# Late routings at six-slot steps, one-hot lists at four-slot steps, V products from group 92, and halved query products in a gather-fed expert stage

## The chip, the cores and the metric

The kernel runs on one core of a Trainium2 chip. The metric is device time in microseconds (us) of one execution. The kernel before took 946.21 us, the median of three runs (945.91 to 949.0).

## The reference, cut to what matters

One decoder layer on 256 tokens of width 1024 in float32: self attention (dilated and block-sparse branches), cross attention, an expert stage, and a final norm. The change is in the expert stage, which is this (heads 8, keys 128, TOPK 16, expert tables of 16384 rows):

```
q = (hf @ w_q).reshape(T, PEER_HEADS, 2, PEER_KEY_DIM // 2)
sc = einsum('thpc,pkc->thpk', q, sub_keys)
v1, i1 = top_k(sc, 16)                  # per half of the key
cand = v1[:, :, 0, :, None] + v1[:, :, 1, None, :]
cidx = i1[:, :, 0, :, None] * 128 + i1[:, :, 1, None, :]
top, pos = top_k(cand, 16)
experts = take_along_axis(cidx, pos)    # 8 heads x 16 experts for each token
gates = softmax(top)
a = gelu(einsum('cd,ced->ce', xc, u[ec]))
y = einsum('ce,ced->cd', gates * a, v[ec])
```

## The kernel before, in words

The first 300 us or so are the attention stages. Then comes the expert stage, which is cut into units, slots and groups. A unit is one head for one tile of 128 tokens (16 units: units 0 to 7 are tile 0). A unit has 16 slots, one for each chosen expert; slot n takes, for every token of the tile, the token's expert row (u and v side by side, 8 KB for each token, 1 MB for a slot) by one indirect DMA that GpSimd issues (line 2385). There are 256 slots. Two slots are a group (128 groups).

A slot goes through these hands. GpSimd waits until the buffer's last user is done (`slot_free`) and issues the gather. VectorE multiplies the u half with the normalised rows and sums it (line 2177, `dot(n)`). ScalarE takes the gelu of a group's two dots, multiplies by the gates and writes two diagonal matrices (lines 1549, 1555 and 1563, `weigh`). TensorE multiplies the diagonals with the v halves, adding into PSUM (`use_pair`, lines 1178 and 1181, with 64x64 tiles), and signals `slot_free`. For the last unit single-slot products are used (lines 1137 and 1300).

The gathers run through a ring of buffers. `ring_order` says which slot uses which buffer. Up to slot 61 there are up to 15 buffers; from `GIVEN_FROM` (62) five are given back for other data. SyncE waits for the last slot in them (`LAST_GIVEN`, line 756) before it sends the expert tables described next.

Experts of the last 20 blocks (of 128 rows each) are not gathered; an index beyond the bound is skipped by the DMA. They are computed densely instead: 20 table blocks of u are multiplied with all tokens' rows (`up_product`, line 1217, groups 37 to 56), and 20 table blocks of v with gated activations (`weigh_block`, line 1249, `DOWN_BEHIND`). The gates for this come from lists: when all routings of a tile are known, TensorE turns the lists (`turn_lists`, lines 1226 and 1227), VectorE splits them (`take_lists`, line 2206 and on), and then for each of 16 chunks of 16 tokens VectorE writes a one-hot array (`onehot`, line 2231), for every second chunk the listed gates (`listed_gates`, lines 2246 and 2251), TensorE multiplies 48 small matrices (`token_gates`, line 1236), ScalarE takes the result (line 1632), and VectorE multiplies it into the activations (`weigh_acts`, line 2260). `weigh_block(0)` waits until all 16 chunks are through. Each v table block is 512 KB, loaded by SyncE when an earlier block has been used; the first five lie ready.

Routing a unit is 15 small VectorE steps (`route_step_of`, lines 1983 to 2055) that are laid behind dots. Which step is behind which slot is written out: `over_slots` for units 1 to 6, `LATE_ROUTES` (first slot of the unit) and `LATE_STEPS` (offset of each step) for units 7 to 15. In late units ScalarE does steps 5, 11 and 15 behind the groups of `RANKS_BEHIND`, `TOP_BEHIND` and `ROWS_BEHIND`. `GATES_AT` says after which slot the gate weights are made.

The query products of heads 3 to 7 are TensorE products of 32 matmuls (`whole_query`, line 836) behind the groups of `QUERY_BEHIND`; two groups later follows `key_score` (line 1147), whose scores routing of that head needs. The score of head 7 is also what SyncE waits for (line 757) before it sends the first u tables.

Programs of all engines are in the order written; an instruction that waits holds all behind it on its engine.

Of the kernel before, what the change touches and what calls it, by code (L numbers as in the profile page):

```python
# [94 lines left out]


EARLY_ROUTED = 6
LATE_ROUTES = {7: 78, 8: 86, 9: 94, 10: 102, 11: 110, 12: 118, 13: 127, 14: 136, 15: 145}
LATE_STEPS = {1: 0, 2: 1, 3: 2, 4: 3, 6: 6, 7: 7, 8: 7, 9: 8, 10: 8, 12: 11, 13: 12, 14: 13}
ROUTE_AT = {}  # L100
for part_of_route in (over_slots(1, 0, 10), over_slots(2, 11, 21), over_slots(3, 29, 39), over_slots(4, 40, 51),
                      over_slots(5, 52, 65), over_slots(6, 66, 79)):
    ROUTE_AT.update(part_of_route)
GATES_AT = {13: 1, 25: 2, 43: 3, 56: 4, 70: 5, 82: 6}
SOFTMAX_BEHIND = {3: 2, 8: 3, 18: 4, 24: 5, 31: 6, 38: 7}
RANKS_BEHIND, TOP_BEHIND, ROWS_BEHIND = {}, {}, {}
for unit, begun in LATE_ROUTES.items():
    for step, at in LATE_STEPS.items():
        ROUTE_AT.setdefault(begun + at, []).append((unit, step))
    RANKS_BEHIND[(begun + 3) // GROUP] = unit  # L110
    TOP_BEHIND[(begun + 8) // GROUP] = unit
    ROWS_BEHIND[(begun + 13) // GROUP] = unit
    GATES_AT[begun + 14] = unit
LAST_ROWS_AT = LATE_ROUTES[UNITS - 1] + 16


TURN_BEHIND = {7: 0, 9: 1}
# [1 line left out]
UP_FROM = 37  # L119
UP_BEHIND = {UP_FROM + b: b for b in range(BLOCKS)}  # L120
TAKE_UP_BEHIND = {UP_FROM + 2 * j + 2: j for j in range(BLOCKS // 2)}
LISTS_BEHIND = {48: 0, 80: 1}
LISTS_AT = {100: 0, 163: 1}
COUNT_AT = 90
ONEHOT_AT = {}
GATHER_GATES_BEHIND = {}
TAKE_GATES_BEHIND = {}
WEIGHTS_AT = {}
for q in range(TOKEN_CHUNKS):
    begun = 114 + 6 * q if q < TOKEN_CHUNKS // 2 else 165 + 7 * (q - TOKEN_CHUNKS // 2) // 2  # L130
    ONEHOT_AT[begun] = q
    GATHER_GATES_BEHIND[(begun + 2) // GROUP] = q
    TAKE_GATES_BEHIND[(begun + 2) // GROUP + 1] = q
    if q % 2:
        WEIGHTS_AT[begun + 8] = q // 2
DOWN_BEHIND = {}
for b in range(BLOCKS):
    DOWN_BEHIND.setdefault(100 + b * 20 // BLOCKS, []).append(b)
PLAIN_GROUPS = (PEER_HEADS * TOPK // GROUP,)
QUERY_BEHIND = {11: 3, 16: 4, 21: 5, 26: 6, 33: 7}  # L140
LAST_SPLIT = PANELS.index("qpeer2")
OWN_PLACE = SPLIT_RING
QUERY_UNITS = PEER_HEADS - QUERIES_FIRST
# [13 lines left out]
FIRST_BUFFERS = [0, 5, 8, 2, 3, 4, 9, 10, 11, 12]  # L157
PRODUCT_BUFFER = 13
JOINS = {22: 14, 24: 15, 58: 6, 67: 7, 79: 1}
GIVEN_BACK, GIVEN_FROM = (10, 11, 12, 14, 15), 62  # L160


def ring_order():
# [62 lines left out]
def product_order():  # L226
# [4 lines left out]
    def add(name, engine):  # L231
        order.append((name, engine))
# [74 lines left out]
    query(2, 1)  # L307

    for i in range(GROUPS):
        if i in QUERY_BEHIND:  # L310
            add(f"qpeer{QUERY_BEHIND[i]}", "act")
        if i - 2 in QUERY_BEHIND:
            add(f"key_score{QUERY_BEHIND[i - 2]}", "act")
        if i in TURN_BEHIND:
            for half in range(2):
                add(f"row_turn{TURN_BEHIND[i]}_{half}", "act")
        if i in UP_BEHIND and UP_BEHIND[i] % 2:
            add(f"up{UP_BEHIND[i] // 2}", "act")
# [40 lines left out]
def build(nc, x_in, mem_in, rel_bias, panels, keys_in, experts, up_in, gain_cols, gain_rows, ident_in,  # L359
          onehot_in, mask_in, iota_in, count_in, out):  # L360
    with ExitStack() as ctx:
# [344 lines left out]
        def _(sp):  # L706
# [45 lines left out]

            sp.wait_ge(product_ready, PLACE["qpeer4"] + 1)
            sp.dma_start(g_final_row, gain_rows[1:2].to_broadcast([P, D])).then_inc(final_row_in, 16)
            sp.wait_ge(slot_free, LAST_GIVEN + 1)
            sp.wait_ge(ffn_sq_ready, 2 * TILES)
            sp.wait_ge(taken["act"], taken_count(f"key_score{PEER_HEADS - 1}"))
            sp.dma_start(count_row[:], count_in.to_broadcast([P, PEER_KEYS])).then_inc(count_in_place, 16)
            for j in range(2 * BLOCKS):
                i = j % len(tables)  # L760
                before = j - len(tables)
                if 0 <= before < BLOCKS and before % 2:
                    sp.wait_ge(product_ready, PLACE[f"up{before // 2}"] + 1)
# [12 lines left out]
        def _(pe):  # L776
# [42 lines left out]
                                           cut(acts_t, slice(None), k, slice(None)), k == 0, k == CHUNKS - 1)  # L819
                mm.then_inc(product_ready, 1)  # L820

            def whole_query(h):

                name = f"qpeer{h}"
                if name in LOADED_EARLY:
                    pe.wait_ge(early_in[name], 16)
                else:
                    i = RAW_LOADED.index(name)
                    pe.wait_ge(panel_in[i % RAW_RING], 16 * (i // RAW_RING + 1))
                w = raw_panel(PANELS.index(name))  # L830
                b = begin(name)
                all_taken("row_turn1_1")
                for blk in range(2):
                    for k in range(CHUNKS):
                        at = k * S + blk * P
                        mm = pe.matmul(b[:, blk * S:(blk + 1) * S], w[:, at:at + P], rowsT[:, k, :],  # L836
                                       start=(k == 0), stop=(k == CHUNKS - 1))
                mm.then_inc(product_ready, 1)

            def tokens_by_channels(name, acts_t):  # L840

# [413 lines left out]
            for i in range(last_unit):  # L1255
                t = i // (GROUPS // TILES)
                if i == 0:
                    query_product(2, 0)
                    for name in LAST_IN_CROSSED:
                        pe.wait_ge(taken[TAKER[name]], taken_count(name))  # L1260
                if i == 4:
                    query_product(2, 1)
                if i in PLAIN_GROUPS:
                    use_group(t, i)
                    pe.wait_ge(crossed_out, 1)
                    first_of_tile = i + 1
                else:
                    use_pair(t, i, i == first_of_tile)
                if i in (0, 5):
                    query_turn(2, i // 5)  # L1270
                if i in (1, 6):
                    query_scores(2, i // 6)
                if i in QUERY_BEHIND:
                    whole_query(QUERY_BEHIND[i])
                if i - 2 in QUERY_BEHIND:
                    key_score(QUERY_BEHIND[i - 2])
                if i in TURN_BEHIND:
                    row_turn(TURN_BEHIND[i])
# [28 lines left out]
        def _(act):  # L1307
# [350 lines left out]
            for i in range((UNITS - 1) * TOPK // GROUP):  # L1658
# [869 lines left out]
```

## Time and profile before

| | |
|---|---|
| median of 3 runs | 946.21 us |
| profiled execution | 948.55 us, of which the span of instructions is 946.8 us |
| TensorE busy | 852.5 us (90%) |
| VectorE busy | 647.8 us (68%) |
| ScalarE busy | 417.6 us (44%) |
| GpSimd busy | 387.2 us (41%) |
| DMA | 303.20 MB, mean 320 GB/s |
| granted TensorE clock, mean | 0.940 |

The span is what lies between the first and the last instruction; the profiled execution's own time is 1.75 us more. Busy shares are means over stages with different limits, so the stretches of the expert stage have to be read one by one. A granted clock of 1.00 is 2.4 GHz, one of 0.50 is 1.2 GHz; a stretch that shows a value between has had both.

### The profile page before, as it was taken

How to read it: one execution, taken by the hardware profiler on the slowest of the kernel's cores; microseconds unless marked ns; L12 is line 12 of the kernel's file. 1: busy time of each engine (PE TensorE's matmuls, PEld its weight loads, DVE VectorE, ACT ScalarE, POOL GpSimd, SP SyncE). 2: the span in 40 equal slices, each digit the busy share in tenths (PEclk: the TensorE clock that was granted, in tenths of full speed). 3: DMA queues.
4: the chain of work that ended last, by engine and by line, in shares of the span. 5: the costliest groups of instructions: out<-in, count | busy, mean ns of one | idle time of the engine just before them, and what ended most of it. 6: DMA issues, size and time to landing. Idle time of an engine off the chain costs nothing.

```text
span 946.8 us, 15680 instructions
## 1 busy us (share of the span) xinstructions
PE 852.5 (90%) x5808; PEld 549.5 (58%) x5808; DVE 647.8 (68%) x1485; ACT 417.6 (44%) x1049; POOL 387.2 (41%) x307
## 2 busy tenths in 40 slices
PE   9999999999988878888779999677897998999997
PEld 8999998899967424444446556333442553333333
DVE  5434685564577876787855787999979775434465
ACT  5534565544664553454434444444452333222252
POOL 1000085150004466465544334455654566444552
PEclk9999999999999879899979999979877788999999
DMA  8897433266328899999999999999999999999995
GB/s 307 236 222 227 175 100 126 90 247 245 138 106 302 317 397 407 399 400 412 347 399 416 416 406 401 371 373 356 325 379 393 381 374 404 418 417 413 405 366 198
DMA packets 55028, 303.20 MB, mean 320 GB/s; under 512 B 11515, under 2 KB 14959, under 8 KB 21777
## 3 DMA queue, kind: packets, MB, share of 16 engines
q0 software_dynamic: 37152, 225.29, 60.2%
q1 hardware_dynamic: 14968, 74.03, 21.5%
q10 hardware_dynamic: 2832, 2.88, 2.1%
q8 instruction: 46, 0.75, 0.3%
q14 instruction: 30, 0.25, 0.1%
HBM read 343.80 MB, written 1.54 MB: 365 GB/s over the span
## 4 chain that ended last, share of the span: by engine, by line
PE 54%; DMA 18%; DVE 16%; issue 5%; ACT 4%; POOL 1%; another core or an unknown queue 1%; POOLq 0%; SPq 0%; DVEq 0%; ACTq 0%
DMA arena<-in_experts,arena 13%; PE y L1178 12%; DVE late_ring L2177 7%; PE ps L792 7%; PE ps L793 7%; PE ps L794 7%; PE y L1249 4%; PE ps L1236 3%; PE ps L836 2%; DMA late_ring<-in_experts,arena 2%; PE y L1137 1%; PE y L1300 1%; PE ps L1217 1%; ACT diag L1563 1%; DMA x<-in_up 1%
## 5 line engine op out<-in xcount | busy, mean ns | idle before, releaser
L2385 POOL DMA_INDIRECT arena<-in_experts,arena x167 | 219.3, 1313 | 170.5 <-PE ps L1181 124.7
L2177 DVE CUSTOM_DVE_ANT_0 late_ring<-arena 128x1024 f32<-128x1024 f32 x178 | 216.7, 1222 | 102.5 <-DMA arena<-in_experts,arena 95.1
L1181 PE MATMUL ps<-arena,diag 64*64 64x512 f32 x824 | 234.5, 697 | 0.2 <-issue 0.2
L1178 PE MATMUL y<-arena,diag 64*64 64x512 f32 x528 | 147.4, 679 | 31.9 <-ACT diag L1563 31.8
L1178 PE MATMUL y<-late_ring,diag 64*64 64x512 f32 x424 | 122.6, 705 | 40.3 <-ACT diag L1563 39.7
L1549 ACT ACTIVATE acts<-dots 128x2 f32<-128x2 f32 x124 | 25.3, 204 | 268.2 <-DVE dots L2177 268.1
L1746 DVE TENSOR_TENSOR w_lo<-raw,w_hi 128x2048 fp32r<-128x2048 f32 x36 | 84.3, 2344 | 70.2 <-ACT w_hi L1329 70.2
L2177 DVE CUSTOM_DVE_ANT_0 late_ring<-late_ring,arena 128x1024 f32<-128x1024 f32 x73 | 89.2, 1222 | 37.5 <-DMA late_ring<-in_experts,arena 26.9
L2385 POOL DMA_INDIRECT late_ring<-in_experts,arena x55 | 71.1, 1292 | 100.2 <-PE ps L1181 90.4
L1178 PEld LDWEIGHTS y<-arena,diag 64*64 64x64 f32 x528 | 35.0, 145 | 112.2 <-ACT diag L1563 56.2
L1178 PEld LDWEIGHTS y<-late_ring,diag 64*64 64x64 f32 x424 | 29.6, 150 | 110.2 <-ACT diag L1563 61.1
L1329 ACT CAST w_hi<-raw 128x2048 fp32r<-128x2048 f32 x37 | 70.7, 1910 | 50.7 <-DMA raw<-in_panels 37.4
L1563 ACT ACTIVATE diag<-ident,acts 128x128 f32<-128x128 f32 x248 | 86.3, 395 | 4.9 <-PE ps L1181 0.8
L792 PE MATMUL ps<-h_hi,w_hi 128*128 128x256 f32 x304 | 86.9, 286 | 0.0
L793 PE MATMUL ps<-h_lo,w_hi 128*128 128x256 f32 x304 | 86.0, 283 | 0.0
L794 PE MATMUL ps<-h_hi,w_lo 128*128 128x256 f32 x304 | 86.0, 283 | 0.0
L2357 POOL TENSOR_SCALAR arena<-arena,row_inv 128x128 f32<-128x128 f32 (+3 forms) x24 | 29.1, 1229 | 115.1 <-DVE row_inv L1814 114.9
L792 PEld LDWEIGHTS ps<-h_hi,w_hi 128*128 128x128 f32 x304 | 58.3, 192 | 2.3 <-issue 1.7
L793 PEld LDWEIGHTS ps<-h_lo,w_hi 128*128 128x128 f32 x304 | 58.3, 192 | 0.0
L794 PEld LDWEIGHTS ps<-h_hi,w_lo 128*128 128x128 f32 x304 | 58.3, 192 | 0.0
L1181 PEld LDWEIGHTS ps<-arena,diag 64*64 64x64 f32 x824 | 56.4, 149 | 0.7 <-issue 0.6
L1555 ACT ACTIVATE acts<-acts,arena 128x1 f32<-128x1 f32 x216 | 52.0, 288 | 4.3
(345 smaller groups left out, 1727.3 us busy)
## 6 DMA issues: line engine op xcount, KB each, us to landing
raw<-in_panels SPq DMA_DIRECT2D x40, 1024.0 KB, 5.0
arena<-in_panels SPq DMA_DIRECT2D x6, 1024.0 KB, 6.9
late_ring<-in_up SPq DMA_DIRECT2D x12, 512.0 KB, 8.5
late_ring<-in_experts SPq DMA_DIRECT2D x12, 512.0 KB, 8.0
x<-in_up SPq DMA_DIRECT2D x8, 512.0 KB, 9.4
x<-in_experts SPq DMA_DIRECT2D x8, 512.0 KB, 7.9
arena<-in_experts,arena POOLq DMA_INDIRECT x167
arena<-line_scratch ACTq DMA_DIRECT2D x8, 320.0 KB, 8.0
```

Of the source, the lines that this page charges most:

```text
L792: pe.matmul(dst, stationary[0], moving[0], start=first, stop=False)
L793: pe.matmul(dst, stationary[0], moving[1], start=False, stop=False)
L794: return pe.matmul(dst, stationary[1], moving[0], start=False, stop=last)
L1178: straight = pe.matmul(y[rows, t, cols], diag[rows, a % DIAGS, rows], slot(a)[rows, down], start=False, stop=False, skip_group_check=True)
L1181: across = pe.matmul(ps[to, half, :], diag[rows, b % DIAGS, rows], slot(b)[rows, down], start=first, stop=False, skip_group_check=True)
L1249: mm = pe.matmul(y[:, t, cols], in_block_acts[:, block, t * P:(t + 1) * P], down[:, cols], start=False, stop=False, skip_group_check=True)
L1329: nc.scalar.copy(split_parts(n)[0], raw_panel(n)).then_inc(w_hi_ready, 1)
L1555: i = nc.scalar.activation(acts[:, s:s + 1], acts[:, s:s + 1], ACT.Copy, scale=gathered_gates(u)[:, s:s + 1])
L1563: i = nc.scalar.activation(diag[:, s % DIAGS, :], ident[:], ACT.Copy, scale=acts[:, s:s + 1])
L1746: nc.vector.tensor_tensor(low, raw_panel(n), high.bitcast(F32), ALU.subtract).then_inc(w_lo_ready, 1)
L2177: i = nc.vector.tensor_tensor_reduce(row if n < len(FIRST_BUFFERS) else products[s % GROUP], row, h_rows[:, u // PEER_HEADS, :], 1.0, 0.0, ...
L2385: nc.gpsimd.indirect_dma_start(out=slot(n), out_offset=None, in_=experts, in_offset=bass.IndirectOffsetOnAxis(ap=expert_rows(u)[:, s:s + 1 ...
```

## The change

Four schedules are altered; no arithmetic is.

1. Late routings (units 7 to 15) begin at slots 77, 83, 89, ... 125, six slots apart, with shorter offsets (the last step at offset 9, before 13). Before they began at 78, 86, ... 145. The groups behind which ScalarE does its part move with them.
2. The lists: turned behind groups 44 and 68 (before 48 and 80), split at slots 93 and 141 (before 100 and 163); the 16 chunks begin at slots 114, 118, ... 174 (before 114, 120, ... 156 and then 165, 168, 172, ... 189).
3. The 20 v blocks lie behind groups 92 to 117, three in four groups (before one behind each of groups 100 to 119).
4. The query products of heads 3 to 7 are cut in halves of 16 matmuls, the first behind a group one earlier than before, the second behind the old one. The scores stay behind the same groups. The five buffers are given back from slot 70 instead of 62, and SyncE waits for them only ahead of the third u table.

```diff
-LATE_ROUTES = {7: 78, 8: 86, 9: 94, 10: 102, 11: 110, 12: 118, 13: 127, 14: 136, 15: 145}
-LATE_STEPS = {1: 0, 2: 1, 3: 2, 4: 3, 6: 6, 7: 7, 8: 7, 9: 8, 10: 8, 12: 11, 13: 12, 14: 13}
+LATE_ROUTES = {unit: 77 + 6 * (unit - EARLY_ROUTED - 1) for unit in range(EARLY_ROUTED + 1, UNITS)}
+LATE_STEPS = {1: 0, 2: 0, 3: 1, 4: 1, 6: 4, 7: 4, 8: 5, 9: 5, 10: 5, 12: 8, 13: 8, 14: 9}
-GATES_AT = {13: 1, 25: 2, 43: 3, 56: 4, 70: 5, 82: 6}
+GATES_AT = {13: 1, 25: 2, 43: 3, 56: 4, 70: 5, 80: 6}
...
-    RANKS_BEHIND[(begun + 3) // GROUP] = unit
-    TOP_BEHIND[(begun + 8) // GROUP] = unit
-    ROWS_BEHIND[(begun + 13) // GROUP] = unit
-    GATES_AT[begun + 14] = unit
-LAST_ROWS_AT = LATE_ROUTES[UNITS - 1] + 16
+    RANKS_BEHIND[(begun + 1) // GROUP] = unit
+    TOP_BEHIND[(begun + 5) // GROUP] = unit
+    ROWS_BEHIND[(begun + 9) // GROUP] = unit
+    GATES_AT[begun + 10] = unit
+LAST_ROWS_AT = LATE_ROUTES[UNITS - 1] + 12
...
-LISTS_BEHIND = {48: 0, 80: 1}
-LISTS_AT = {100: 0, 163: 1}
+LISTS_BEHIND = {44: 0, 68: 1}
+LISTS_AT = {93: 0, 141: 1}
...
-    begun = 114 + 6 * q if q < TOKEN_CHUNKS // 2 else 165 + 7 * (q - TOKEN_CHUNKS // 2) // 2
+    begun = 114 + 4 * q
...
-    DOWN_BEHIND.setdefault(100 + b * 20 // BLOCKS, []).append(b)
+    DOWN_BEHIND.setdefault(92 + b * 27 // BLOCKS, []).append(b)
-QUERY_BEHIND = {11: 3, 16: 4, 21: 5, 26: 6, 33: 7}
+QUERY_BEHIND = {10: 3, 15: 4, 20: 5, 25: 6, 32: 7}
-GIVEN_BACK, GIVEN_FROM = (10, 11, 12, 14, 15), 62
+GIVEN_BACK, GIVEN_FROM = (10, 11, 12, 14, 15), 70
...
-            sp.wait_ge(slot_free, LAST_GIVEN + 1)
...
             for j in range(2 * BLOCKS):
                 i = j % len(tables)
+                if j == TILES:
+                    sp.wait_ge(slot_free, LAST_GIVEN + 1)
...
-            def whole_query(h):
+            def half_query(h, blk):
...
-                b = begin(name)
+                b = bank(name) if blk else begin(name)
                 all_taken("row_turn1_1")
-                for blk in range(2):
-                    for k in range(CHUNKS):
+                for k in range(CHUNKS):
...
-                mm.then_inc(product_ready, 1)
+                if blk:
+                    mm.then_inc(product_ready, 1)
...
                 if i in QUERY_BEHIND:
-                    whole_query(QUERY_BEHIND[i])
-                if i - 2 in QUERY_BEHIND:
-                    key_score(QUERY_BEHIND[i - 2])
+                    half_query(QUERY_BEHIND[i], 0)
+                if i - 1 in QUERY_BEHIND:
+                    half_query(QUERY_BEHIND[i - 1], 1)
+                if i - 3 in QUERY_BEHIND:
+                    key_score(QUERY_BEHIND[i - 3])
```

ScalarE's `take_query` and `take_scores` move by one index as well, so that they stay behind the same groups.

## Rows read from the trace of the kernel before

**Rows 1.** The page, part 2: 40 slices of 23.67 us.
```profile
PEclk9999999999999879899979999979877788999999
GB/s 307 236 222 227 175 100 126 90 247 245 138 106 302 317 397 407 399 400 412 347 399 416 416 406 401 371 373 356 325 379 393 381 374 404 418 417 413 405 366 198
```
**Rows 2.** Busy time by stretch: from:to, length, PE PEld DVE ACT POOL, PEclk, DMA share, GB/s.
```profile
440.00:480.00 40.00, 27.00 (x180) 11.55 (x172) 30.39 (x83) 18.52 (x55) 24.37 (x17) 0.89 0.94 362
480.00:590.00 110.00, 105.25 (x598) 66.88 (x602) 76.94 (x246) 44.98 (x135) 43.45 (x38) 0.98 1.02 412
590.00:646.00 56.00, 43.25 (x344) 21.17 (x344) 55.08 (x158) 25.95 (x84) 27.04 (x21) 0.88 0.96 361
646.00:694.00 48.00, 35.70 (x311) 16.44 (x304) 47.65 (x127) 23.77 (x74) 27.77 (x21) 0.82 0.95 360
694.00:757.00 63.00, 55.14 (x494) 27.97 (x497) 52.60 (x93) 21.77 (x79) 33.60 (x26) 0.76 0.98 380
757.00:801.00 44.00, 39.16 (x368) 19.72 (x360) 30.52 (x48) 14.02 (x50) 28.78 (x21) 0.85 0.97 386
801.00:903.00 102.00, 100.12 (x437) 35.51 (x434) 44.57 (x74) 25.45 (x93) 48.32 (x37) 0.99 1.01 412
```
**Rows 3.** The dots alone (line 2177) by stretch, two instructions for each slot.
```profile
589.90:645.70 55.80, 28.15 (x46) 0.88 0.96 362
645.70:694.40 48.70, 24.31 (x40) 0.82 0.95 359
694.40:756.90 62.50, 32.25 (x54) 0.76 0.98 381
```
**Rows 4.** VectorE's groups of instructions by shape, 589.9 to 684.2 us.
```profile
L2231 DVE TENSOR_TENSOR late_ring<-counts,column_of 128x2048 bf16<-128x2048 bf16 x7 | 8.5, 1216 | 0.0
L2047 DVE TENSOR_TENSOR work<-work,pairs 128x800 f32<-128x800 f32 x5 | 4.9, 989 | 0.0
...
L2260 DVE TENSOR_TENSOR late_ring<-late_ring,gate_sums 128x640 f32<-128x640 f32 x2 | 3.0, 1480 | 0.0
L2251 DVE TENSOR_TENSOR gates_even<-raw,gate_piece 128x640 bf16<-128x640 bf16 x6 | 2.6, 487 | 0.1
...
L2246 DVE TENSOR_TENSOR raw<-raw,row_of 128x640 bf16<-128x640 bf16 x4 | 2.0, 491 | 0.0
```
**Rows 5.** VectorE's waits, 690 to 800 us: in total, times, longest.
```profile
DVE late_ring L2231 <- remote: 4.6, 1, 4.6
DVE late_ring L2231 <- PE ps L1236: 4.5, 1, 4.5
DVE gate_rest L2206 <- PE ps L1227: 3.9, 1, 3.9
```
**Rows 6.** Timeline of TensorE: start, us, line, [idle before <-releaser].
```profile
457.82 7.17 PE L836 MATMUL ps<-rowsT,arena 128*128 128x256 f32 x32
...
481.94 5.07 PE L1217 MATMUL ps<-rowsT,x 128*128 128x256 f32 x16 [5.25 <-DMA x<-in_up]
...
598.76 0.60 PE L1178 MATMUL y<-late_ring,diag 64*64 64x512 f32 x2
...
719.81 1.06 PE L1178 MATMUL y<-late_ring,diag 64*64 64x512 f32 x2
...
726.83 3.19 PE L1236 MATMUL ps<-gates_even,late_ring 128*128 128x20 bf16 x48
```
**Rows 7.** Timeline of GpSimd, behind the query product of head 7.
```profile
467.70 1.05 POOL L2385 DMA_INDIRECT arena<-in_experts,arena  x1 [5.79 <-PE ps L1181]
```
**Rows 8.** The chain that ended last, in order of time, its end.
```profile
902.93 3.63 PE y L1249 x8
906.56 0.58 PE y L1178 x2
908.44 3.63 PE y L1249 x8
912.07 6.87 PE y L1137 x16
```
**Rows 9.** The page, part 3: GpSimd's DMA queue.
```profile
q0 software_dynamic: 37152, 225.29, 60.2%
```
**Rows 10.** Two stretches of 20 us, columns as in rows 2.
```profile
580.00:600.00 20.00, 17.15 (x104) 10.41 (x96) 16.91 (x51) 8.81 (x26) 7.81 (x6) 1.00 1.01 405
...
820.00:840.00 20.00, 20.00 (x93) 6.90 (x91) 7.89 (x15) 4.15 (x15) 9.28 (x8) 1.00 1.02 417
```

More of the change, by code:

```diff
@@ L309, in product_order @@
     for i in range(GROUPS):
-        if i in QUERY_BEHIND:
-            add(f"qpeer{QUERY_BEHIND[i]}", "act")
-        if i - 2 in QUERY_BEHIND:
-            add(f"key_score{QUERY_BEHIND[i - 2]}", "act")
+        if i - 1 in QUERY_BEHIND:
+            add(f"qpeer{QUERY_BEHIND[i - 1]}", "act")
+        if i - 3 in QUERY_BEHIND:
+            add(f"key_score{QUERY_BEHIND[i - 3]}", "act")
         if i in TURN_BEHIND:
@@ L830, in whole_query @@
                 w = raw_panel(PANELS.index(name))
-                b = begin(name)
+                b = bank(name) if blk else begin(name)
                 all_taken("row_turn1_1")
-                for blk in range(2):
-                    for k in range(CHUNKS):
-                        at = k * S + blk * P
-                        mm = pe.matmul(b[:, blk * S:(blk + 1) * S], w[:, at:at + P], rowsT[:, k, :],
-                                       start=(k == 0), stop=(k == CHUNKS - 1))
-                mm.then_inc(product_ready, 1)
+                for k in range(CHUNKS):
+                    at = k * S + blk * P
+                    mm = pe.matmul(b[:, blk * S:(blk + 1) * S], w[:, at:at + P], rowsT[:, k, :],
+                                   start=(k == 0), stop=(k == CHUNKS - 1))
+                if blk:
+                    mm.then_inc(product_ready, 1)
             def tokens_by_channels(name, acts_t):
@@ L1273, in _ @@
                 if i in QUERY_BEHIND:
-                    whole_query(QUERY_BEHIND[i])
-                if i - 2 in QUERY_BEHIND:
-                    key_score(QUERY_BEHIND[i - 2])
+                    half_query(QUERY_BEHIND[i], 0)
+                if i - 1 in QUERY_BEHIND:
+                    half_query(QUERY_BEHIND[i - 1], 1)
+                if i - 3 in QUERY_BEHIND:
+                    key_score(QUERY_BEHIND[i - 3])
                 if i in TURN_BEHIND:
@@ L1680, in _ @@
                     take_scores_tile(2, 1)
-                if i - 2 in QUERY_BEHIND:
-                    take_query(QUERY_BEHIND[i - 2])
                 if i - 3 in QUERY_BEHIND:
-                    take_scores(QUERY_BEHIND[i - 3])
+                    take_query(QUERY_BEHIND[i - 3])
+                if i - 4 in QUERY_BEHIND:
+                    take_scores(QUERY_BEHIND[i - 4])
                 if i in TAKE_TURN_BEHIND:
```

## The prediction

> **What bounds the kernel now.** I read the page's slices first, then busy time by stretch, then the dots alone, then the waits and timelines of the places that stood out. In the slices [rows 1] the gathers run near 400 to 418 GB/s from slice 15 on, with three dents: slice 19 (347), slices 26 to 29 (371, 373, 356, 325), and a long shallow one up to slice 34. The best 20 us show 417 GB/s [rows 10], and I take that as what the transfers can do. The stretches [rows 2] say what stands behind each dent.
> - 440 to 480: 362 GB/s. No engine is full. TensorE is busy 27 of 40 us, the ring is short, and GpSimd waits 5.79 us for buffers behind the query product of head 7 [rows 7], which holds TensorE for 7.17 us [rows 6].
> - 480 to 590: 412 GB/s, TensorE 105 of 110 us. Transfers and TensorE both bind, VectorE does not (77 of 110).
> - 590 to 694: 360 GB/s, and VectorE busy 102.7 of 104 us. VectorE alone binds: dots, routings and lists lie on one another. The gathers lose (1 - 360/417) x 104 = 14 us here.
> - 694 to 757: 380 GB/s, TensorE 55 of 63 us at a granted clock of 0.76, VectorE 52.6. Here VectorE waits 3.9 us for the turned lists and 4.5 us for a one-hot's buffer; another 4.6 us follow [rows 5].
> - 757 to 801: 386 GB/s. 801 to 903: 412 GB/s and TensorE 100 of 102 us. Both bind again. The chain's end is TensorE without a gap: v blocks of 3.63 us and pairs, then the last unit [rows 8].
>
> So time is what the gathers need plus what they lose. One slot is 225.29 MB / 256 = 0.880 MB [rows 9], or 2.14 us at 412 GB/s. A slot can't be faster than this except out of what is already landed.
>
> **Unit prices.** Between 589.9 and 645.7 us there are 46 dot instructions, so slots 114 to 136 (23 slots) took 55.8 us; the next 20 took 48.7 and the next 27 took 62.5 [rows 3]. A dot costs 28.15/23 = 1.22 us, and about 1.135 from start to start, as its neighbours overlap it by 0.08 to 0.09. By the same overlap a one-hot is 1.13 us, listed gates (one product and three, 0.49 each) 1.7, a weighing 1.40 [rows 4]. A chunk of a list is 1.13 + 1.7/2 + 1.40/2 = 2.68 us. In the VectorE-bound part a slot costs (55.8 + 48.7)/43 = 2.43 us. With a chunk each six slots (0.45) and a routing each eight to nine, this leaves 0.85 a slot, 7.1 us for one late routing; its three products over 800 elements alone are 2.7 [rows 4].
>
> **The change part by part.**
>
> *Ring and halved queries (440 to 480).* The halves put 16 matmuls (3.6 us) behind each of two groups instead of 7.17 behind one. With the later give-back, slots 66 to 78 have 11 to 14 slots between reuses of a buffer, before 9 to 11. The most this can return is the whole loss, (1 - 362/417) x 40 = 5.3 us; the least is nothing, as head 7's scores stay behind group 35 and with them the send of the first u table, whose late landing holds TensorE 5.25 us [rows 6]. The SyncE wait that moves behind two tables was over by then anyway. Earlier queries lie where slices show 397 to 412 GB/s [rows 1] and can give little. I take -3, nearer the upper end, because both causes named in the rows are treated.
>
> *More routing between slots 80 and 114.* From slot 114 on there were 5.0 routings left (0.3 of unit 10, 0.7 of unit 11, units 12 to 15). Now 3.3 are left (0.45 of unit 12, 0.87 of 13, units 14 and 15). So 1.7 x 7.1 = 12 us move forward into the stretch where VectorE has 33 us free of 110 [rows 2]: 89 of 110. Costs lie between 0 and 3 us (a pair that gets steps 3, 4, 12 and 13 needs 2.3 + 1.4 + 1.8 = 5.5 us, just the 5.5 of a group there). I take +1, as the gathers are the bound.
>
> *Slots 114 to 136.* Now: 23 dots 26.1, 3.3 routings 23.4, six one-hots 6.8, three listed gates 5.1 and the fixed rows 0.5, two weighings 2.8: 64.7 us. The same count for before is 26.1 + 2.6 x 7.1 + 4.5 + 3.4 + 0.5 + 1.4 = 54.4, against 55.8 measured, so 1.4 go on top: 66. This stretch gets 10 us longer, a VectorE-bound 2.87 us a slot. Bounds: +6 if the gathers' lead at its start hides part, +14 if ScalarE's casts (three places a unit, now two slots from their users instead of three) are late once or more.
>
> *Slots 137 to 183.* Before 48.7 + 62.5 = 111.2 us. No routing is left here. VectorE has 47 dots 53.3, the lists' split 2, ten one-hots 11.3, five listed gates 8.5, six weighings 8.4: 83.5 us, under the gathers' 47 x 2.14 = 100.6. What is late next is the transfer. The waits of 3.9 and 4.5 us go: the lists are turned four to five slots ahead of the split (before two to three), and a one-hot comes five slots behind the group that frees its buffer (the waiting ones had four). Bounds: 111.2 - 97 = -14 with three landed slots used up, and -2.4 if the pace stays at 62.5/27 = 2.31. I take -11, nearer to the transfer's own row. This and the part before make -1.
>
> *v products, slots 184 to 239.* In 757 to 903 the core moved 44 x 386 + 102 x 412 = 59.0 MB [rows 2]. The same at 412 throughout is 143 us against 146, at 417 it is 141.5. TensorE needs 28 pairs x 1.75 (four starts 0.43 apart, [rows 8]) plus 20 x 3.63 = 122 us, and has gaps again. The 4.6 us wait [rows 5] is in this stretch and goes as well. Bounds 0 and -8 (57.1 MB of 56 slots and 15 tables alone are 138.7 us). I take -4.
>
> *The end.* The last unit's products no longer stand behind a 3.63 us block [rows 8]. The last gathers wait on them: 0 to -3.6, I take -1, since the last dots wait for rows.
>
> Sum: -3 + 1 + 10 - 11 - 4 - 1 = -8 us. The profiled execution (span 946.8, its own time 948.55) would become 938.8 and 940.5. The profiled one is 2.3 us above the median of the runs, so the median goes from 946.2 to **938 us**.
>
> **Two rules of the Trainium skill.** GpSimd issued 21 gathers in 27.04 us in the VectorE-bound 590 to 646 and 37 in 48.32 in the calm 801 to 903: 1.29 and 1.31 us each [rows 2]. The Trainium skill, "SBUF — State Buffer" (Door 3 and the warning on SWDGE under it), says that GpSimd can't write DMA descriptors while VectorE runs a two-port operation. By that rule, packing one-hots and routings closer would slow the gathers' issue; these rows show no longer issue where VectorE is full. I give it nothing.
>
> **The rivals.**
> 1. *Slower: the clock falls in the v stretch.* v blocks now leave every fourth group bare, and TensorE waits for rows there. Where TensorE was busy 39 of 44 us the clock was 0.85, and 0.76 in the stretch before it [rows 2]; pairs then take 1.06 instead of 0.60 us each [rows 6]. TensorE's work for groups 92 to 117 is 26 x 1.75 + 20 x 3.63 = 118 us at full clock, the gathers' 52 x 2.14 + 19 = 130. It decides from a mean clock of 118/130 = 0.91 downward. At 0.80, the mean of the two rows, it is 148 us, 18 more than forecast: 956. Against it: with u blocks between pairs and TensorE busy only 17.15 of 20 us the clock was 1.00 [rows 10], and here it would be about 0.9 busy. Chance 0.12. The Trainium skill, "TensorE: Matmul & The Clock Gate" (HAM oscillation), has this mechanism: idle gaps put the array back to half rate. By that rule the time would come out near rival 1's; the rows of 580 to 600 speak against gaps that long.
> 2. *Same: the middle gives back what the end wins.* Landed rows don't help, one-hots still wait for TensorE at five slots (at clock 0.76 two pairs and 48 small matmuls are 2 x 3.5 + 3.2 = 10.2 us of the 10.7 that five slots last), and slots 137 to 183 run at 2.31. Then -2.4 instead of -11, with the rest at -3: about 945. For it: all three waits of [rows 5] are of that kind. Chance 0.16.
> 3. *Much faster.* Every upper bound but one: -5 + 0 + 7 - 12 - 6 - 2 = -18, 928 us. For it: 14 us lost in 590 to 694 alone. Against: the dense stretch makes a loss of its own. Chance 0.18.
>
> That the schedule isn't kept (a routing or list late, so that a later unit's gathers wait) would be seen as GpSimd waiting for expert rows. The last routing ends near slot 135 and is used from slot 240; nothing there is tight.
>
> **How the numbers follow.** The forecast has 0.54, with a range of its own from 930 to 946. With the rivals, 926 to 949 leaves out under 0.2: the clock case above (0.12) and a third of rival 3 below (0.06). What a measurement can tell is 0.3%, 2.8 us. Faster than 943.4: 0.54 x 0.88 + 0.18 + a little of rival 2 = 0.67. Within: 0.18. Slower than 949: 0.15.
>
> **What would show it.** Right, step by step: no wait over 3 us for the query of head 7 and over 400 GB/s in 440 to 470; VectorE near full over slots 114 to 136 only, about 66 us long; slots 137 to 183 in about 100 us with VectorE under 90% and no wait over 3 us for lines 2206 and 2231; slots 184 to 239 at 410 GB/s with a clock of 0.95 or more. Wrong: a clock of 0.8 behind group 92; one-hots waiting over 4 us in several places; or a longer dense stretch, with casts on ScalarE as the releaser.

## The result: 0.4% slower, outside the forecast

The changed kernel takes 951.27 us (median of 16 runs, 948.15 to 956.1), the kernel before 948.0 us on the same chips (16 runs, 943.9 to 952.51). The ratio is 1.0041, 95% interval 1.0025 to 1.0058. The forecast was 938 us, 8 faster. The profiled execution took 950.01 us, its span 948.2.

The page's slices of the changed kernel (23.7 us each), beside [rows 1]:

```profile
PEclk9999999999999999999989999777879799999999
...
GB/s 306 235 203 228 189 98 133 90 229 260 137 109 295 343 421 416 395 417 418 363 409 407 412 410 390 332 297 268 365 410 409 409 407 417 416 412 372 403 375 186
```

Counted from 0, the dent at slice 19 is shallower (363, before 347). The dent of the middle (slices 25 to 28; the prediction's "26 to 29" are the same four) has become much deeper: 332, 297, 268, 365 where there were 371, 373, 356, 325. Behind it all is at 407 to 417 up to slice 35.

To compare two schedules I cut both traces at the same dots, not at the same times: at the starts of the 115th, 138th, 153rd, 185th and 241st dot (slots 114, 137, 152, 184, 240). Busy time by these stretches, first the kernel before, then the changed one (from:to, length, PE PEld DVE ACT POOL, PEclk, DMA share, GB/s):

```profile
590.00:645.70 55.70, 42.95 (x342) 20.92 (x342) 54.78 (x157) 25.65 (x84) 26.74 (x21) 0.88 0.96 362
645.70:684.20 38.50, 29.14 (x272) 14.59 (x264) 38.22 (x107) 17.81 (x57) 23.20 (x18) 0.87 0.93 344
684.20:757.00 72.80, 62.01 (x534) 30.07 (x538) 62.33 (x115) 28.04 (x97) 38.46 (x30) 0.75 0.99 385
757.00:903.30 146.30, 139.58 (x801) 55.39 (x794) 75.09 (x121) 39.73 (x144) 77.10 (x58) 0.95 1.00 404
```

```profile
585.80:653.10 67.30, 53.28 (x421) 27.19 (x420) 66.27 (x180) 32.05 (x97) 31.91 (x23) 0.77 0.88 322
653.10:686.30 33.20, 33.20 (x306) 17.45 (x305) 30.49 (x58) 11.06 (x39) 19.84 (x14) 0.80 0.86 319
686.30:760.10 73.80, 64.47 (x631) 34.39 (x629) 55.77 (x88) 25.55 (x91) 51.22 (x35) 0.84 1.01 408
760.10:905.60 145.50, 131.02 (x607) 44.69 (x608) 69.12 (x112) 38.87 (x142) 71.40 (x56) 0.95 1.00 404
```

The first dot is at 304.7 and 305.6 us, so the two run alike up to there. Then, by slots:

| slots | before | changed | difference | forecast |
|---|---|---|---|---|
| 0 to 113 | 285.3 | 280.2 | -5.1 | -2 |
| 114 to 136 | 55.7 | 67.3 | +11.6 | +10 |
| 137 to 151 | 38.5 | 33.2 | -5.3 | |
| 152 to 183 | 72.8 | 73.8 | +1.0 | |
| (137 to 183) | 111.3 | 107.0 | -4.3 | -11 |
| 184 to 239 | 146.3 | 145.5 | -0.8 | -4 |
| 240 to 254 | 33.4 | 33.5 | +0.1 | -1 |

The fuller stretch came as forecast; what was to pay for it did not. All three waits of [rows 5] are gone. What VectorE still waits for in 690 to 800 us is rows that the gathers have not yet landed, and it waits for them longer: 37.0 us in all. In the kernel before it was 10.4 us.

```profile
DVE late_ring L2177 <- DMA arena<-in_experts,arena: 9.8, 10, 1.2
DVE late_ring L2177 <- DMA late_ring<-in_experts,arena: 0.6, 1, 0.6
```

```profile
DVE late_ring L2180 <- DMA arena<-in_experts,arena: 30.6, 26, 2.0
DVE late_ring L2180 <- DMA late_ring<-in_experts,arena: 6.4, 6, 1.4
```

So 13 us of waits were removed, and waits for rows took their place: slots 152 to 183, which held two of the three, did not get shorter. That is what the experiments are about. Line numbers of the changed kernel are one to three higher (the dot is line 2180).

### The profile page after: what moved, and what is told of

Read it like the earlier page. It is cut to its first block, busy times and chain, and to the rows that moved or that the text cites. A ratio compares the mean times of both kernels' runs of the same rounds, so it can differ in the third digit from the quotient of the medians.

```text
span 948.2 us, 15693 instructions
## 1 busy us (share of the span) xinstructions
PE 853.0 (90%) x5808; PEld 548.6 (58%) x5808; DVE 652.1 (69%) x1485; ACT 415.0 (44%) x1049; POOL 397.2 (42%) x307
## 4 chain that ended last, share of the span: by engine, by line
PE 50%; DMA 24%; DVE 12%; ACT 6%; issue 5%; POOL 3%; POOLq 0%; SPq 0%; DVEq 0%; ACTq 0%
DMA late_ring<-in_experts,arena 11%; PE y L1179 10%; DMA arena<-in_experts,arena 9%; PE ps L793 6%; PE ps L794 6%; PE ps L795 6%; PE ps L1218 6%; DVE late_ring L2180 4%; PE y L1250 3%; DMA late_ring<-in_experts,expert 2%; POOL arena L2388 2%; PE ps L836 2%; DVE w_lo L1749 1%; ACT diag L1566 1%; ACT w_hi L1332 1%
## 5 line engine op out<-in xcount | busy, mean ns | idle before, releaser
L2388 POOL DMA_INDIRECT arena<-in_experts,arena x164 | 226.6, 1382 | 226.6 <-PE ps L1182 181.5
L1179 PE MATMUL y<-arena,diag 64*64 64x512 f32 x784 | 218.5, 685 | 51.1 <-ACT diag L1566 51.0
L1179 PEld LDWEIGHTS y<-arena,diag 64*64 64x64 f32 x784 | 52.0, 147 | 171.5 <-ACT diag L1566 88.1
L1182 PE MATMUL ps<-arena,diag 64*64 64x512 f32 x544 | 145.7, 661 | 0.0
L1749 DVE TENSOR_TENSOR w_lo<-raw,w_hi 128x2048 fp32r<-128x2048 f32 x36 | 84.9, 2360 | 73.7 <-ACT w_hi L1332 73.7
L2180 DVE CUSTOM_DVE_ANT_0 late_ring<-late_ring,arena 128x1024 f32<-128x1024 f32 x75 | 91.8, 1223 | 41.2 <-DMA late_ring<-in_experts,arena 33.7
L1182 PE MATMUL ps<-late_ring,diag 64*64 64x512 f32 x408 | 116.5, 697 | 0.0
L2388 POOL DMA_INDIRECT late_ring<-in_experts,arena x58 | 78.5, 1354 | 34.2 <-PE ps L1182 17.4
L2360 POOL TENSOR_SCALAR arena<-arena,row_inv 128x128 f32<-128x128 f32 (+3 forms) x24 | 25.7, 1084 | 120.2 <-DVE row_inv L1817 119.9
L1179 PE MATMUL y<-late_ring,diag 64*64 64x512 f32 x168 | 44.5, 654 | 18.5 <-ACT diag L1566 18.5
L1250 PE MATMUL y<-late_ring 128*128 128x512 f32 x96 | 45.6, 619 | 0.0
```

The costliest lines, as they stand in the source:

```text
L1179: straight = pe.matmul(y[rows, t, cols], diag[rows, a % DIAGS, rows], slot(a)[rows, down], start=False, stop=False, skip_group_check=True)
L1182: across = pe.matmul(ps[to, half, :], diag[rows, b % DIAGS, rows], slot(b)[rows, down], start=first, stop=False, skip_group_check=True)
L1250: mm = pe.matmul(y[:, t, cols], in_block_acts[:, block, t * P:(t + 1) * P], down[:, cols], start=False, stop=False, skip_group_check=True)
L1749: nc.vector.tensor_tensor(low, raw_panel(n), high.bitcast(F32), ALU.subtract).then_inc(w_lo_ready, 1)
L2180: i = nc.vector.tensor_tensor_reduce(row if n < len(FIRST_BUFFERS) else products[s % GROUP], row, h_rows[:, u // PEER_HEADS, :], 1.0, 0.0, ...
L2388: nc.gpsimd.indirect_dma_start(out=slot(n), out_offset=None, in_=experts, in_offset=bass.IndirectOffsetOnAxis(ap=expert_rows(u)[:, s:s + 1 ...
```

## The experiments

Each ratio is to the kernel before, run on the same chip in the same rounds, with its 95% interval. The changed kernel itself was not run in these rounds, so a comparison with it is one of two ratios, or of stretches. How far two ratios can be trusted is seen from e12 below: its edit brought about none of the waits that it was made for, and it is at 1.0005 where the changed kernel is at 1.0041. Differences of whole times under some 4 us can't be told this way, except between kernels of the same rounds (e7 and e8, e13 and e14). Stretches are from one profiled execution each. Theory D: the density of slots 114 to 136 is the loss. Its rivals are named with each run.

### Front part alone (e1_queries)

The changed kernel with routings, lists and v products as before:

```diff
-LATE_ROUTES = {unit: 77 + 6 * (unit - EARLY_ROUTED - 1) for unit in range(EARLY_ROUTED + 1, UNITS)}
+LATE_ROUTES = {7: 78, 8: 86, 9: 94, 10: 102, 11: 110, 12: 118, 13: 127, 14: 136, 15: 145}
...
-    begun = 114 + 4 * q
+    begun = 114 + 6 * q if q < TOKEN_CHUNKS // 2 else 165 + 7 * (q - TOKEN_CHUNKS // 2) // 2
```

> Theory D (density: the change lost because routings every six slots and list chunks every four lie on one another over slots 114 to 136, and TensorE works off the backlog at a low clock behind it): the halved queries and the later give-back alone are a small gain, 1 to 4 us under the kernel before, as slots up to 114 came 4.2 us earlier in the changed kernel. Theory Q (the front part of the change costs): at or above the kernel before.

946.73 us, ratio 0.9983 (0.9963 to 1.0003). Not clear of no change, but hardly a cost; theory Q is not borne out. Slots 114 to 183 are as before (56.2, 38.6, 72.6 us).

### v products back (e2_v_back)

```diff
-    DOWN_BEHIND.setdefault(92 + b * 27 // BLOCKS, []).append(b)
+    DOWN_BEHIND.setdefault(100 + b * 20 // BLOCKS, []).append(b)
```

> The changed kernel with its v products back behind groups 100 to 119. Theory D: v products from group 92 were no harm, so this is 0 to 4 us slower than the changed kernel, 950 to 955. Theory V (leaving every fourth group bare and starting at 92 is what lost: 4.0 us of transfers are lost over slots 200 to 240 against 1.6 before): 3 us or more faster than the changed kernel, at or under the kernel before.

950.46 us, ratio 1.0023 (1.0000 to 1.0046), which can't be told from the changed kernel's 1.0041. Slots 184 to 239 take 145.5 us, the very number of the changed kernel. Where the v products lie makes neither a gain (my -4) nor a loss (theory V) that can be seen.

### Routings and front part, no lists (e3_routes_queries)

The changed kernel with lists and v products as before.

```diff
-LISTS_AT = {93: 0, 141: 1}
+LISTS_AT = {100: 0, 163: 1}
...
-    begun = 114 + 4 * q
+    begun = 114 + 6 * q if q < TOKEN_CHUNKS // 2 else 165 + 7 * (q - TOKEN_CHUNKS // 2) // 2
```

> The changed kernel with lists and v products as before, so routings every six slots and the queries alone. Theory D: slots 114 to 136 take about 61 us (56 before, 67 changed), slots 137 to 156 are lighter than in both, and the waits of 3.9, 4.5 and 4.6 us stand: 942 to 946. If routings alone are the harm (theory R: ScalarE's casts, VectorE in 80 to 114): at or above the changed kernel.

947.98 us, ratio 0.9990 (0.9967 to 1.0013), 2 us above the expected band. Slots 114 to 136 took 61.8 us (expected 61), 137 to 151 36.6, 152 to 183 72.2. The waits did not stand as expected: in 690 to 805 us VectorE waits once for TensorE, 1.6 us, at line 2234. Theory R, that routings alone are the harm, falls; a gain isn't shown either.

With e1 and e2 this splits the change in two. The routings (e1 to e3) add 5.6 us to slots 114 to 136 and take 2.0 off slots 137 to 151. The lists (e3 to e2) add 5.4 and take 3.0 off. Neither takes anything from slots 152 to 183 (72.6, 72.2, 72.8).

### First chunks sparse (e4_first_sparse)

```diff
-    begun = 114 + 4 * q
+    begun = 114 + 6 * q if q < 4 else 138 + 4 * (q - 4)
...
-    DOWN_BEHIND.setdefault(92 + b * 27 // BLOCKS, []).append(b)
+    DOWN_BEHIND.setdefault(97 + b * 23 // BLOCKS, []).append(b)
```

> The changed kernel with the first four list chunks six slots apart (114 to 132), the others four apart from 138 to 182, v products behind groups 97 to 119. Theory D: slots 114 to 136 take 60 to 62 us and lose 10 us of transfers instead of 15; over all 4 to 7 us faster than the changed kernel, 944 to 947. Theory V or R: no better than the changed kernel by more than 1 us.

944.09 us, ratio 0.9964 (0.9945 to 0.9984). Slots 114 to 136 took 61.8 us instead of 67.3, and what follows is not slower for it: 33.8, 72.8, 145.4. Moving two of six chunks out of the full stretch (the v products moved as well, which e2 shows to be no matter) turns the slower kernel into one faster than before. This is theory D's case, by size too.

### A third of TensorE's list work (e5_one_piece)

```diff
-                    for piece in range(PIECES):
+                    for piece in range(1):
...
```

> The changed kernel, but TensorE multiplies only the first of three gate pieces for the lists (16 small matmuls a chunk, not 48; two thirds of each gate's precision is left out), so a chunk holds TensorE some 1.1 us instead of 3.2. VectorE's work is the same. Theory P (behind slot 137 TensorE's backlog is what delays the buffers): slots 137 to 151 lose 3 us of transfers or less instead of 7.8, slots 114 to 136 stay at 67 us, in all 4 to 7 us faster than the changed kernel. Theory S (only VectorE's excess counts and the ring just refills): slots 137 to 151 still lose 7 us, at most 1 us faster.

947.0 us, ratio 0.9974 (0.9957 to 0.9991), 4 us under the changed kernel by the medians, 6 by the ratios, 3 by the stretches. Slots 114 to 136 are unchanged (67.2), 137 to 151 go from 33.2 to 30.3 us:

```profile
652.40:682.70 30.30, 25.10 (x200) 11.17 (x196) 30.06 (x58) 10.93 (x39) 20.63 (x14) 0.84 0.94 345
```

In the changed kernel TensorE was busy all of these 33.2 us at a clock of 0.80 and VectorE 30.5; now VectorE has 30.06 of 30.3. Theory P is right in kind: behind the full stretch TensorE's backlog matters. But it is 3 us, not 5: of 417 GB/s the stretch still loses 5.2 us of transfers, between theory P's 3 and theory S's 7. Slots 152 to 183 take 73.7 us again, so nothing of TensorE's list work mattered there.

### Less one-hot work on VectorE (e6_no_onehot)

```diff
-                nc.vector.tensor_tensor(onehots[q % 2], counts[:],
+                few = PEER_KEYS if q < 2 else 4
+                nc.vector.tensor_tensor(onehots[q % 2][:, 0:few, :], counts[:, 0:few, :],
```

> The changed kernel, but from the third chunk on VectorE writes only 4 of 128 columns of the one-hot array (the rest of it is left out and stays old), about 1 us less for each of 14 chunks; TensorE's work is the same. Theory P: slots 114 to 136 get 4 us shorter, slots 137 to 151 still lose 6 us or more, as TensorE has the same backlog; about 4 us faster in all. Theory S: both stretches get better, 137 to 151 lose 4 us or less; 7 us faster or more.

947.3 us, ratio 0.9982 (0.9957 to 1.0007). Slots 114 to 136 took 63.1 us, 4.2 less for four one-hots, so each us of VectorE work in this stretch is a us of time. 137 to 151: 31.7. Of the 10 one-hots behind slot 137 the four in this stretch gave 1.5 us, the six in 152 to 183 nothing (74.1). By the stretches it is 5 us faster than the changed kernel, and 137 to 151 still lose 5.8 us of transfers (theory P: about 4, and 6 or more). That is near theory P; the whole time, 6 us faster by the ratios, would not by itself rule out theory S's 7.

### Routings at five slots, two list schedules (e7_routes5_sparse, e8_routes5_dense)

If VectorE's work is dear in slots 114 to 136 and free before, more of the routing belongs before.

```diff
-LATE_ROUTES = {unit: 77 + 6 * (unit - EARLY_ROUTED - 1) for unit in range(EARLY_ROUTED + 1, UNITS)}
-LATE_STEPS = {1: 0, 2: 0, 3: 1, 4: 1, 6: 4, 7: 4, 8: 5, 9: 5, 10: 5, 12: 8, 13: 8, 14: 9}
+LATE_ROUTES = {unit: 77 + 5 * (unit - EARLY_ROUTED - 1) for unit in range(EARLY_ROUTED + 1, UNITS)}
+LATE_STEPS = {1: 0, 2: 0, 3: 1, 4: 1, 6: 4, 7: 4, 8: 5, 9: 5, 10: 5, 12: 8, 13: 8, 14: 8}
...
-    GATES_AT[begun + 10] = unit
+    GATES_AT[begun + 9] = unit
...
-LISTS_BEHIND = {44: 0, 68: 1}
-LISTS_AT = {93: 0, 141: 1}
+LISTS_BEHIND = {44: 0, 64: 1}
+LISTS_AT = {93: 0, 133: 1}
```

e7 has chunks and v products of e4 besides, e8 those of the changed kernel.

> Late routings five slots apart (77 to 117, their last three steps behind one slot), the second list split at slot 133, the first four chunks six slots apart and the others four, v products behind groups 97 to 119. Theory D: VectorE's sum over slots 114 to 136 is 53 us, under before's 54, as the routings move on into slots 80 to 113, which are bound by transfers (lost there: 3 to 5 us). Slots 114 to 136 take 55 us, and the whole is 4 to 7 us faster than with six-slot routings: 938 to 941. Theory R (more routing before 114 costs as much there): 944 or more.

> The changed kernel with late routings five slots apart and the second list split at slot 133; chunks every four slots and v products as in the changed kernel. Theory D: VectorE's sum over slots 114 to 136 is 58 us instead of 65, so it takes 60 us; 5 to 7 us faster than the changed kernel, 944 to 946, and slower than the sparse one of this call by 3 us or more. Theory R: as the changed kernel.

e7: **941.19 us, ratio 0.9903 (0.9879 to 0.9927)**. e8: 945.66 us, ratio 0.9961 (0.9941 to 0.9981). Both came out as theory D expected, e7 0.2 us above its 938 to 941; between the two lie 4.5 us for two chunks. e7 is faster than both kernels. Its four stretches:

```profile
588.60:644.20 55.60, 42.77 (x331) 20.36 (x332) 54.31 (x137) 28.08 (x86) 26.75 (x19) 0.85 0.89 329
644.20:679.60 35.40, 30.89 (x330) 17.05 (x323) 28.68 (x43) 10.61 (x38) 24.38 (x19) 0.95 1.00 409
679.60:751.90 72.30, 65.05 (x629) 34.36 (x628) 59.40 (x93) 24.71 (x88) 45.04 (x32) 0.83 0.98 395
751.90:897.00 145.10, 130.35 (x655) 47.13 (x654) 70.52 (x116) 40.19 (x146) 70.79 (x56) 0.95 1.00 402
```

The first stretch is as short as before, with VectorE at its limit in it alone; the second has the transfers at 409 GB/s. The slots ahead, which got the work, took 282.0 us (280.2 in the changed kernel).

### Three chunks ahead of slot 138 (e11_three_first)

e7 with `begun = 114 + 8 * q if q < 3 else 138 + 4 * (q - 3)` and v products from group 99.

> Routings five slots apart as in the best so far (which has four chunks before slot 138 and is at 0.990 of before), with only three chunks before slot 138 (eight slots apart), thirteen from 138 to 186, v products behind groups 99 to 119. Theory D: VectorE's sum over slots 114 to 136 falls from 53 to 50 us, near the transfers' 49; 1 to 3 us better, 938 to 940. Theory F (what is left there is the ring's own): no better than 941.

941.19 us, ratio 0.9906 (0.9882 to 0.9931): no better than e7. Slots 114 to 136 took 56.1 us with VectorE busy 53.2, only 1.1 less than in e7, where 3 less were expected. The outcome is theory F's (at 53 us of VectorE work the stretch isn't VectorE's any more), but as VectorE's work hardly fell, the run decides little.

### Fewer bytes (e9_half_tables, e10_fewer_rows)

```diff
-                sp.dma_start(tables[i], table).then_inc(table_in[i], 16)
+                cols = slice(0, D if j < BLOCKS else D // 2)
+                sp.dma_start(tables[i][:, cols], table[:, cols]).then_inc(table_in[i], 16)
```

```diff
-                    bounds_check=GATHERED - 1, oob_is_err=False,
+                    bounds_check=GATHERED - 11 * P - 1, oob_is_err=False,
...
```

> The changed kernel, but the 20 v tables are loaded only in their first half of columns (the other half stays as it was and is left out), 3.9 MB less over slots 184 to 239; TensorE multiplies as before. Theory M (transfers set slots 184 to 239, wherever the v products lie): 145.5 us become 136 to 139. Theory E (TensorE or the ring's round trip sets it): 143 or more.

> The changed kernel, but 11 further blocks of experts (10% of the gathered ones) are neither gathered nor weighed (left out), every instruction else the same; a slot moves 0.79 MB, not 0.88. Theory M (slots 152 to 183 and 184 to 239 are bound by transfers): 73.8 becomes 66 to 69 and 145.5 becomes 134 to 138, while slots 114 to 136, bound by VectorE, stay at 67. Theory E: under 2 us less in each.

942.2 us, ratio 0.9900 (0.9862 to 0.9938), and 919.16 us, ratio 0.9671 (0.9641 to 0.9702). Their last stretches, slots 184 to 239 of e9, then slots 114 to 239 of e10:

```profile
762.00:898.30 136.30, 127.36 (x606) 43.97 (x608) 69.11 (x112) 38.95 (x143) 72.59 (x56) 0.97 1.00 399
```

```profile
575.20:642.40 67.20, 57.15 (x440) 29.68 (x439) 66.16 (x180) 33.32 (x101) 33.33 (x24) 0.82 0.87 315
642.40:674.60 32.20, 32.16 (x324) 17.76 (x324) 30.24 (x56) 10.96 (x39) 20.48 (x15) 0.89 0.82 288
674.60:743.00 68.40, 59.94 (x629) 33.63 (x627) 55.55 (x89) 25.33 (x91) 50.88 (x34) 0.90 0.98 383
743.00:877.00 134.00, 124.78 (x590) 43.34 (x591) 68.99 (x112) 38.60 (x141) 73.27 (x56) 0.97 1.00 394
```

Theory M in every number: 136.3 and 134.0 (changed: 145.5), 68.4 (73.8), and 67.2 where VectorE binds (67.3). Slots 152 to 239 follow the bytes. For slots 152 to 183 this rests on e10 alone, and fewer bytes also shorten the way of each single gather; that the transfers' rate is the limit there, and not this way, is argued from a DMA share of 0.98 to 1.01 in most runs.

### Two waits (e12_two_waits)

`begun = 114 + 4 * q - (2 if q in (11, 15) else 0)`: two one-hots nearer to the group that frees their buffer.

> The changed kernel with chunks 11 and 15 two slots early (156 and 172), three slots behind the group that frees their buffer, so that VectorE waits 3 to 5 us for TensorE at each. Theory M: slots 152 to 183 are set by transfers and still take 73 to 74 us, the whole is within 1 us of the changed kernel. Theory W (as I forecast, such waits are lost time): 5 us or more slower there.

950.81 us, ratio 1.0005 (0.9986 to 1.0024), slots 152 to 183 in 72.2 us. Inconclusive: the waits did not arise. In 690 to 800 us VectorE waited for rows (34.4 us) and for nothing of TensorE's. So the waits had to be made certain.

### Certain waits, late and early (e13_waits_late, e14_waits_dense)

e13 waits at gathers 157 and 171, e14 at 119 and 131 instead:

```diff
+                if n in (157, 171):
+                    dve.wait_ge(slot_free, n + 1)
```

> The changed kernel with two added waits of VectorE for TensorE's use of the slot just multiplied, behind slots 157 and 171, each 4 to 6 us long. Theory M (transfers set the pace over slots 152 to 183, a wait of VectorE under the ring's slack is free): slots 152 to 183 take 73 to 76 us, the whole at most 2 us over the changed kernel. Theory W (such waits are lost time, as I forecast): 82 us or more there.

> The changed kernel with the same two waits behind slots 119 and 131, where VectorE binds. Both theories: slots 114 to 136 get 8 to 12 us longer, from 67 to 75 to 79. Theory M: slots 137 to 183 get back at most 3 us of it, so the whole is 6 us or more over the changed kernel.

e13: 952.92 us, ratio 1.0049 (1.0025 to 1.0073), against the changed kernel's 1.0041. e14: 956.24 us, ratio 1.0073 (1.0050 to 1.0096). The waits are there, and larger in e13; first its two, then its slots 152 to 183 (start, us, instruction, [idle before]):

```profile
705.34 1.23 DVE L2180 CUSTOM_DVE_ANT_0 late_ring<-arena 128x1024 f32<-128x1024 f32 x1 [3.70 <-PE ps L1182]
...
740.87 1.23 DVE L2180 CUSTOM_DVE_ANT_0 late_ring<-arena 128x1024 f32<-128x1024 f32 x1 [7.15 <-PE ps L1182]
```

```profile
688.50:762.90 74.40, 64.47 (x598) 34.03 (x601) 55.11 (x89) 24.61 (x88) 44.08 (x31) 0.82 0.95 377
```

10.9 us of waits lengthen this stretch by 0.6 us. They take the place of waits for rows: VectorE waits 5.7 us for rows in this stretch, and 17.3 in the changed kernel. They may not be wholly free: the next 56 slots take 146.6 us (145.5) and slots 240 to 254 35.0 (33.5), 3 us in all in this profile, which is of one of the longer executions (955.46 us); the medians differ by 1.7 us. In e14, 8.9 us of waits (4.46 and 4.39) lengthen slots 114 to 136 by 8.9, from 67.3 to 76.2:

```profile
588.40:664.60 76.20, 56.11 (x438) 28.29 (x440) 66.31 (x180) 32.06 (x98) 31.24 (x23) 0.73 0.80 293
664.60:695.50 30.90, 30.90 (x300) 16.55 (x296) 30.21 (x58) 10.93 (x40) 19.69 (x14) 0.83 0.89 332
```

The stretch behind gives back 2.3 and the next 1.5. That is 3.8 where at most 3 were expected, and the whole is 5 us over the changed kernel by the medians and by the stretches, 3 by the ratios, where 6 or more were expected: a miss in size. The contrast is theory M's all the same: the same kind of wait costs its full length in the one stretch and a twentieth in the other, and e14, with the smaller waits, is 3.3 us slower than e13 in the same rounds.

All stretches by slots, in us, one profiled execution each:

| kernel | 114 to 136 | 137 to 151 | 152 to 183 | 184 to 239 |
|---|---|---|---|---|
| before | 55.7 | 38.5 | 72.8 | 146.3 |
| changed | 67.3 | 33.2 | 73.8 | 145.5 |
| e1, front alone | 56.2 | 38.6 | 72.6 | 144.8 |
| e2, v back | 67.2 | 33.6 | 72.8 | 145.5 |
| e3, routings and front | 61.8 | 36.6 | 72.2 | 145.0 |
| e4, first chunks sparse | 61.8 | 33.8 | 72.8 | 145.4 |
| e5, a third of list work | 67.2 | 30.3 | 73.7 | 145.6 |
| e6, short one-hots | 63.1 | 31.7 | 74.1 | 145.6 |
| e7, five slots, sparse | 55.6 | 35.4 | 72.3 | 145.1 |
| e8, five slots, dense | 61.3 | 34.8 | 72.6 | 146.1 |
| e9, half v tables | 67.2 | 33.5 | 72.9 | 136.3 |
| e10, a tenth fewer rows | 67.2 | 32.2 | 68.4 | 134.0 |
| e11, three first | 56.1 | 34.6 | 73.5 | 144.9 |
| e12, two waits | 67.2 | 34.4 | 72.2 | 145.9 |
| e13, waits late | 67.2 | 34.2 | 74.4 | 146.6 |
| e14, waits dense | 76.2 | 30.9 | 72.3 | 145.5 |

## Why the prediction was wrong

Step by step, as it put them.

**Front, to slot 113 (-3, +1): right in sign, small.** -5.1 in these profiles. GpSimd's wait about head 7's query is 3.42 and 2.55 us in two parts instead of 5.79 [rows 7], and 440 to 480 us is at 386 GB/s (362), not over 400 as foreseen. Ten profiled kernels with these queries and six-slot routings (e10 left aside) take 279.6 to 282.8 us for this part, so one profile is good to some 3 us here, and e1's whole is -1.6 (+-2) us by the ratio. The 12 us of routing moved here cost little if anything: e1, without them, takes 281.5 us, and in the changed kernel 480 to 586 us is at 405 GB/s with VectorE busy 88 of 106 us.

**Slots 114 to 136 (+10): right.** +11.6. The count of VectorE's work made 66 us, 67.3 were measured, and the same recipe gave e3, e4, e8 and e7 within 2 us. For e11 it missed VectorE's busy time by 3. GpSimd took 31.91 us for 23 gathers here, 1.39 each, against 26.74 for 21, 1.27 each, before: the issue did get longer with the closer packing, but GpSimd was busy under half of the stretch, so this set nothing. (Nothing here shows that the one-hots, TENSOR_TENSOR in [rows 4], are two-port operations, as the prediction's use of its rule takes them to be.)

**Slots 137 to 183 (-11): this failed.** It was -4.3. I wrote "The waits of 3.9 and 4.5 us go" and "What is late next is the transfer", and counted the stretch down to 2.14 us a slot. The failed step is this price: it takes the waits for time that comes back, and the transfers for running at full rate with nothing to make up, from slot 137 on. Three things were wrong in it.
- *The waits cost next to nothing where they stood.* Slots 152 to 183 take 72.2 to 74.4 us in the kernel before and in all variants with the full bytes, whether VectorE waits 8.4 us in them for TensorE (before), 10.9 (e13) or not at all. Less waiting for TensorE is more waiting for rows: 1.5 us before, 5.7 in e13, 17.3 in the changed kernel. e10 shows that bytes move it. (No run takes the waits alone out of the kernel before.) In [rows 2], 694 to 757 has a DMA share of 0.98 with VectorE at 52.6 of 63: the row said it, and I read 380 GB/s as loss to be got back.
- *The transfers had a reserve to make up.* I took the mean of all slots, 0.880 MB, at 412 GB/s. In slots 152 to 183 the core moved 408 GB/s x 73.8 us = 30.1 MB for these 32 slots, 0.94 MB each. The excess went into rows not yet used. At slot 128, VectorE-bound, a gather was issued 20.7 us ahead of its dot, at slot 137 16.5, at slot 152 8.5, at slot 180 13.8. So it is not the full stretch that drains the ring but slots 137 to 151: at 33.2 us they look near 15 x 2.14 = 32.1, but the transfers ran at 319 GB/s there, and the dots lived on rows landed before. Gathers issued and not yet multiplied were 7 at the start of slot 137, 5 at slot 152 and 7 at slot 184; in the kernel before 5, 7 and 4. That kernel moved less in slots 152 to 183 (385 GB/s) and drew three gathers from the reserve; the changed one moved more and put two back. Why both come to 73 us, no run here tells.
- *TensorE's backlog.* Slots 137 to 151 had VectorE busy 30.5 of 33.2 us but TensorE all of it, at a clock of 0.80, and it signals buffers free only when it is through. e5, with a third of the list products, takes 3 us less. How much of the backlog is work and how much is the clock, which had been granted at half speed around slot 137, no run separates:

```profile
652.00:655.00 3.00, 3.00 (x37) 2.24 (x38) 2.97 (x8) 2.03 (x8) 1.70 (x2) 0.50 0.98 339
655.00:660.00 5.00, 5.00 (x30) 1.54 (x26) 4.96 (x10) 0.86 (x4) 0.02 (x1) 0.57 0.76 300
```

Rival 2 had the pace (2.31 us a slot; it was 107.0/47 = 2.28), but by one-hots that wait for TensorE, and no one-hot waited. TensorE held up the buffers instead.

**v products (-4): failed.** -0.8. Slots 184 to 239 take 144.8 to 146.6 us in every kernel with the full bytes, with v blocks from group 92, 97, 99 or 100, and 136.3 with 3.9 MB less. It was transfer-bound before the change; I priced it at a rate (412 to 417) that no schedule reached over the whole stretch (398 to 409 GB/s). The 4.6 us wait of this stretch went too, and the stretch got 0.8 us shorter.

**The clock (rival 1): did not come.** Bare groups leave the clock at 0.95 over slots 184 to 239, as before. Where the clock did fall is earlier: 0.77 over slots 114 to 136 (0.88 before) and 0.80 over 137 to 151 (0.87).

The direction follows. The change moved 12 us of routing ahead of slot 114, where it cost little. But into slots 114 to 136, where VectorE is full and every us counts, it drew 0.7 of a routing (5 us) and two more list chunks (5.4 us), out of slots 137 to 183. There the routings and lists had cost far less than their length, as e1, e2 and e3 show (11.0 us more in the one stretch, 5.0 less in the other), and the waits next to nothing. Rival 2 (945, "the middle gives back what the end wins") was nearest, yet on the wrong side as well.

## What to carry to other kernels

Cut both traces at the same work items, not at the same times, and ask for each stretch whether it follows bytes, an engine's sum, or neither, before pricing a wait in it: an engine's wait in a stretch that follows the bytes is worth next to nothing, and a us of work in a stretch where the engine is full is a us. Move work from the full stretch to the transfer-bound one ahead of it (e7), and don't bring other work into the full one. After a stretch that starved the transfers, count what they have to make up before the slots get faster.

## What the runs showed that I had not expected

Two stretches kept their time over all variants of the schedule within 3%: 32 slots in 72.2 to 74.4 us and 56 slots in 144.8 to 146.6 us. The last 15 dots took 33.4 to 34.1 us in all but e13 (35.0). VectorE at 88 of 106 us beside bound transfers cost them at most little (405 GB/s against 412), and in e7, with 96.7 of 108.6 us, no more (406).
